# Rounding normalised feature tiles from the banks and sharing the normalisation between VectorE and ScalarE

## The chip, the core and the metric

The kernel runs on one core of a Trainium2 chip. The time is the device time of one launch in microseconds; it is read as the median of several runs. The engines have short names: PE (TensorE, matmuls and transposes; PEld are its weight loads), DVE (VectorE), ACT (ScalarE), POOL (GpSimd), SP (SyncE, which issues most DMAs). SBUF is the on-chip memory, and PE writes into eight banks of 128x512 f32.

## The reference

Two residual layers of an encoder, over 512 tokens (4 tiles of 128) with 1024 features (8 feature tiles of 128), all in f32:

```
for layer in range(2):
    mix = even_mixer(x) if layer == 0 else odd_mixer(x)      # GLA + windowed attention / gated DeltaNet
    x = layer_norm(ALPHA * x + mix, ln1_g, ln1_b)
    x = layer_norm(ALPHA * x + (silu(x @ w_gate) * (x @ w_up)) @ w_down, ln2_g, ln2_b)

def layer_norm(x, g, b):
    mu = mean(x); xc = x - mu
    return xc * rsqrt(mean(xc * xc) + 1e-5) * g + b
```

Each mixer is an input projection, the recurrence or attention, and an output projection of 1024 x 1024; the feed-forward width is 2816.

## The kernel before

Every f32 product is made of three matmuls: an operand is cut into a rounded high part and the low part that is left (x = x_hi + x_lo, w = w_hi + w_lo), and PE adds hi·hi, hi·lo and lo·hi into one bank (`mm3`). Weights come in blocks of 1 MB into two buffers `w_raw`; ACT rounds a block to `w_hi` in two pieces (line 823), POOL subtracts for `w_lo` in two pieces (line 681). Each engine has its own program in written order, and they meet at semaphores only: `full(e, key)` waits for a bank to be filled (on DVE and ACT it drains the engine first), `taken` for a bank to have been read.

Around a layer norm (i = 1, 2, 3; the fourth ends the kernel) there is a handover:

1. As PE finishes each token tile t of the last product, DVE adds it to ALPHA·x in `x_tm` (line 1234), takes statistics (1236, 1216), ACT takes the root (839), DVE the reciprocal (1191), and DVE normalises the row's two halves (1207). The normalising of a tile stands behind the adding of the next one.
2. PE transposes the four tiles into eight banks ("xT", i, k), one per feature tile k (`turn_x`, line 1816).
3. The norm's g and b are applied per feature as scale and bias. ACT makes x_hi of k = 0 from its bank (line 830). For every k, DVE writes f_ab, the unrounded feature tile, into one of four buffers (line 1174); for k = 1 to 7 ACT rounds x_hi from f_ab (line 834). The low part f_ab - x_hi is made by DVE for even k (line 1164) and by POOL for odd k (line 688).
4. `fm_block(..., fresh=i)` is PE's first weight block after the norm, two output tiles n: for each k, hi·hi and hi·w_lo for both n (1695, 1696), then the products with x_lo two tiles behind (1700). The banks of the two outputs are those of k = 1 and k = 0.

Before step 3, ACT rounds the next weight block (`split_to(... + 1)`), and POOL makes the first half of its w_lo ahead of the odd low parts, the second half behind them. After layer norm 2, ACT issues three DMAs between the two, among them `ba_w`, which PE needs in `few_columns` (line 1722) right after the fresh block. After a handover POOL also brings x_tm to the normalised x·g + b, one token tile in each of four weight blocks (794, 797), while SP loads the blocks that follow.

The end of a mixer: tiles 0 to 2 of the output projection's first half fill gaps of the mixer (`FILLERS`, `TAIL_FILLERS`, `LAST_FILLERS`). In layer 0 the last two fillers are done with k = 0 to 3 as `part_of` (high parts first, then the products with w_lo), k = 4 to 7 with `tile_of` (all three products at each k, so that each waits for w_lo). Then the last token tile is transposed (`turn_o`, line 1830). In layer 1 the filler `ahead` is cut in pieces around the transposes of the last OO, which DVE scales head by head (line 1634). The second half of the projection follows as `tm_group(("mix", layer, 1))`.

Of the kernel before, what the change touches and what calls it, by code (L numbers as in the profile page):

```python
# [286 lines left out]
def trunk_kernel(nc, A, out):  # L287
# [8 lines left out]
    with ctx:  # L296
# [31 lines left out]
        rstd = sb("rstd", [P, NT])  # L328
        TH = NT * GDN_H
# [181 lines left out]
        for b, (name, k0, nk, width, _) in enumerate(blocks):  # L511
# [19 lines left out]
            "eye_landed", "x_landed", "ln_landed", "warm_ready", "w_first_hi", "w_first_lo", "x_hi_ready", "x_lo_even", "x_lo_odd", "z_norm", "half_stats", "ln_stat", "ln_var",  # L531
# [143 lines left out]
        def _(pool):  # L675
# [8 lines left out]
            def low_parts(i):  # L684

                for k in range(1, KD, 2):
                    pool.wait_ge(s["x_hi_ready"], KD * i + k + 1)
                    pool.tensor_tensor(x_lo[:, k, :], f_ab[:, k % 4, :], x_hi[:, k, :].bitcast(F32), ALU.subtract)\
                        .then_inc(s["x_lo_odd"], 1)
# [74 lines left out]
            for b in range(2, NB):  # L764
# [39 lines left out]
        def _(act):  # L804
# [21 lines left out]
            def round_x(i):  # L826
# [151 lines left out]
            split_to(first_block[("gate", 0, 0)] + 1)  # L978
            round_x(1)
# [4 lines left out]
            split_to(first_block[("conv", KD)] + 1)  # L984
# [5 lines left out]
            round_x(2)  # L990
# [138 lines left out]
            split_to(first_block[("gate", 1, 0)] + 1)  # L1129
            round_x(3)  # L1130
# [6 lines left out]
        def _(dve):  # L1137
# [19 lines left out]
            def round_x(i):  # L1157
# [9 lines left out]
                for k in (1, 0, *range(2, KD)):  # L1167
                    full(dve, ("xT", i, k))
                    if k == 0:
                        dve.wait_ge(s["x_hi_ready"], KD * i + 1)  # L1170
# [5 lines left out]
                    if k % 2 == 0 and k > 0 or k == KD - 1:  # L1176
                        low((k - 1) // 2 * 2)
# [9 lines left out]
            def layer_norm(i, group, layer):  # L1187

                def normalise(t):
# [447 lines left out]
            filler(NT - 1, 3)  # L1637
# [10 lines left out]
        def _(pe):  # L1648
# [35 lines left out]
            def fm_block(b, keys, fresh=None, width=P):  # L1684
# [3 lines left out]
                for k in range(KD) if fresh is not None else ():  # L1688
# [38 lines left out]
            def tm_group(name, wait_k, src=xcols, kt=KD, in_turn=False, tiles=range(NT), pair_last=False):  # L1727
# [3 lines left out]
                while b < NB and blocks[b][0] == name:  # L1731
# [6 lines left out]
                    waited = -1  # L1738
                    for kk, t in steps:
# [470 lines left out]
```

## Time and profile before

| | us |
|---|---|
| median of 3 runs | 1258.07 (1258.04 to 1260.04) |
| the profiled execution's own time | 1257.68 |
| its span in the trace | 1255.87 |
| PE busy | 1232.8 |
| POOL, DVE, ACT busy | 602.8, 449.1, 442.0 |

The page shows one execution. Busy time counts an engine's instructions; a wait is shown in brackets as idle time before an instruction with what released it. The chain that ended last consists of PE by 91%, so the places that matter are those where PE waits.

### The profile page before, as it was taken

The page shows a single profiled execution, that of the slowest core. Times are in us where ns is not written, and L with a number is a line of the kernel's source. Part 1 is how long each engine was busy: PE and PEld are TensorE (multiplying, and loading weights), DVE is VectorE, ACT ScalarE, POOL GpSimd, SP SyncE. Part 2 cuts the span into 40 slices and gives each one's busy share as a digit, 9 for nine tenths or more (in the row PEclk, how much of TensorE's full clock was granted, in tenths as well). Part 3 has the DMA queues.
Part 4 walks back from the last instruction along what each step waited for, and adds up shares of the span by engine and source line. Part 5 has one row for each costly group of instructions (what it writes and reads, how often), then busy time and mean ns, then how long its engine had stood idle before and what let it go on. Part 6 is the DMA issues. An engine that isn't in the chain of part 4 may idle for free.

```text
span 1255.9 us, 17125 instructions
## 1 busy us (share of the span) xinstructions
PE 1232.8 (98%) x7112; PEld 1011.2 (81%) x7112; DVE 449.1 (36%) x769; ACT 442.0 (35%) x661; POOL 602.8 (48%) x292
## 2 busy tenths in 40 slices
PE   9999998999999999999999999999999999999997
PEld 7878776888888888886777889887688888888885
DVE  5557526311111000127778845663621111010105
ACT  4167724222222221214544456542422222221111
POOL 4243444944444343446743347444694444435341
PEclk9999999999999999999999999999999999999999
DMA  9221041333233233231344243124133233323231
GB/s 321 91 68 68 23 147 44 124 102 99 75 97 98 87 126 124 101 101 48 103 116 120 75 127 94 27 69 134 34 107 109 86 101 101 101 84 135 83 101 67
DMA packets 106065, 122.96 MB, mean 98 GB/s; under 512 B 18947, under 2 KB 80581, under 8 KB 105989
## 3 DMA queue, kind: packets, MB, share of 16 engines
q1 hardware_dynamic: 98244, 118.56, 29.7%
q10 hardware_dynamic: 7744, 3.32, 1.0%
q8 instruction: 56, 0.92, 0.3%
q14 instruction: 21, 0.16, 0.0%
HBM read 117.93 MB, written 3.70 MB: 97 GB/s over the span
## 4 chain that ended last, share of the span: by engine, by line
PE 91%; DVE 4%; DVEq 2%; POOL 1%; issue 1%; ACT 1%; ACTq 0%
PE bank L1661 27%; PE bank L1663 27%; PE bank L1662 27%; PE bank L2062 3%; DVEq L471 2%; DVE f_ab L1174 1%; POOL w_lo L681 1%; DVE stats L1236 1%; DVE x_tm L1234 1%; PE bank L2171 1%; PE bank L1722 1%; PE bank L1894 1%; PE bank L2008 0%; PE bank L2154 0%; DVE x_tm L1197 0%
## 5 line engine op out<-in xcount | busy, mean ns | idle before, releaser
L681 POOL TENSOR_TENSOR w_lo<-w_raw,w_hi 128x1024 fp32r<-128x1024 f32 (+1 forms) x200 | 469.9, 2371 | 525.7 <-ACT w_hi L823 525.5
L1661 PE MATMUL bank<-x_hi,w_hi 128*128 128x512 f32 x880 | 344.3, 391 | 0.0
L1662 PE MATMUL bank<-x_lo,w_hi 128*128 128x512 f32 x880 | 342.5, 389 | 0.0
L1663 PE MATMUL bank<-x_hi,w_lo 128*128 128x512 f32 x880 | 342.5, 389 | 0.0
L823 ACT ACTIVATE w_hi<-w_raw 128x1024 fp32r<-128x1024 f32 (+1 forms) x200 | 196.3, 1032 | 210.0 <-issue 161.3
L1661 PEld LDWEIGHTS bank<-x_hi,w_hi 128*128 128x128 f32 x880 | 165.2, 188 | 35.2 <-issue 0.8
L1663 PEld LDWEIGHTS bank<-x_hi,w_lo 128*128 128x128 f32 x880 | 165.2, 188 | 34.4
L1662 PEld LDWEIGHTS bank<-x_lo,w_hi 128*128 128x128 f32 x880 | 165.2, 188 | 34.0
L1243 DVE TENSOR_TENSOR f_ab<-bank,f_ab 128x512 f32<-128x512 f32 x44 | 30.4, 692 | 363.7 <-PE bank L1663 363.7
L1663 PE MATMUL bank<-w_hi,h_lo 128*128 128x512 f32 x352 | 136.9, 389 | 0.0
L1661 PE MATMUL bank<-w_hi,h_hi 128*128 128x512 f32 x352 | 136.9, 389 | 0.0
L1662 PE MATMUL bank<-w_lo,h_hi 128*128 128x512 f32 x352 | 136.9, 389 | 0.0
L1661 PE MATMUL bank<-w_hi,x_hi 128*128 128x512 f32 (+1 forms) x312 | 121.9, 391 | 2.1 <-POOL w_lo L681 2.1
L1663 PE MATMUL bank<-w_hi,x_lo 128*128 128x512 f32 (+1 forms) x312 | 118.4, 379 | 0.0
L1662 PE MATMUL bank<-w_lo,x_hi 128*128 128x512 f32 (+1 forms) x312 | 118.2, 379 | 0.0
L1234 DVE SCALAR_TENSOR_TENSOR x_tm<-x_tm,bank 128x512 f32<-128x512 f32 x32 | 22.0, 688 | 251.4 <-PE bank L1663 249.8
L862 ACT ACTIVATE h_hi<-f_ab 128x512 fp32r<-128x512 f32 x44 | 27.8, 632 | 187.4 <-DVE f_ab L1243 187.4
L1661 PEld LDWEIGHTS bank<-w_hi,h_hi 128*128 128x128 f32 x352 | 66.1, 188 | 13.8
L1662 PEld LDWEIGHTS bank<-w_lo,h_hi 128*128 128x128 f32 x352 | 66.1, 188 | 13.7
L1663 PEld LDWEIGHTS bank<-w_hi,h_lo 128*128 128x128 f32 x352 | 66.1, 188 | 13.7
L857 ACT ACTIVATE f_ab<-bank 128x512 f32<-128x512 f32 x44 | 26.3, 598 | 142.9 <-PE bank L1663 140.5
L1661 PEld LDWEIGHTS bank<-w_hi,x_hi 128*128 128x128 f32 x312 | 58.7, 188 | 15.4 <-POOL w_lo L681 3.8
(284 smaller groups left out, 1243.3 us busy)
## 6 DMA issues: line engine op xcount, KB each, us to landing
w_raw<-ffn_w_gate_dram SPq DMA_DIRECT2D x22, 1024.0 KB, 5.4
w_raw<-ffn_w_up_dram SPq DMA_DIRECT2D x22, 1024.0 KB, 5.3
w_raw<-ffn_w_down_dram SPq DMA_DIRECT2D x20, 1024.0 KB, 5.0
w_raw<-od_w_in_dram SPq DMA_DIRECT2D x16, 1024.0 KB, 5.9
w_raw<-ev_w_in_dram SPq DMA_DIRECT2D x8, 1024.0 KB, 5.6
w_raw<-ev_w_out_dram SPq DMA_DIRECT2D x4, 1024.0 KB, 5.2
w_raw<-od_w_out_dram SPq DMA_DIRECT2D x4, 1024.0 KB, 5.2
x_fm<-x_fm_dram SPq DMA_DIRECT2D x8, 256.0 KB, 6.8
```

What stands on the lines that cost most here:

```text
L471: e.drain()
L681: pool.tensor_tensor(w_lo[:, b % 2, c], w_raw[:, b % 2, c], w_hi[:, b % 2, c].bitcast(F32), ALU.subtract).then_inc(w_lo_ready, 1)
L823: act.activation(w_hi[:, i % 2, c], w_raw[:, i % 2, c], ACT.Copy).then_inc(w_hi_ready, 1)
L857: take(act.activation(f_ab[:, j, :], bank(("gate", layer, f + j))[:, :], ACT.Silu), ("gate", layer, f + j))
L862: act.activation(h_hi[:, f + j, :], f_ab[:, 2 + j, :], ACT.Copy).then_inc(s["h_hi_ready"], 1)
L1174: take(dve.tensor_scalar(f_ab[:, k % 4, :], src, lnc[:, gcol + k:gcol + k + 1], lnc[:, gcol + 16 + k:gcol + 17 + k], ALU.mult, ALU.add), ( ...
L1234: take(dve.scalar_tensor_tensor(cols, cols, ALPHA, bank(key)[:, :], ALU.mult, ALU.add), key)
L1243: take(dve.tensor_tensor(f_ab[:, 2 + f % 2, :], bank(("up", layer, f))[:, :], f_ab[:, f % 2, :], ALU.mult), ("up", layer, f))
L1661: pe.matmul(out_ap, st[0], mv_[0], start=start, stop=False)
L1662: pe.matmul(out_ap, st[0], mv_[1], start=False, stop=False)
L1663: return pe.matmul(out_ap, st[1], mv_[0], start=False, stop=stop)
L2062: return pe.matmul(o, a, b_, start=True, stop=True)
```

## The change

ACT reads the banks itself for k = 2 to 7 and makes x_hi from them (its own scale and bias); it also writes f_ab for k = 3, 5, 7, while DVE writes it for k = 1 and the even k only, each followed at once by its low part. ACT normalises the second half of every token tile, with a factor -mean·rstd that DVE computes into `nm_rstd`; the transposes of k = 4 to 7 wait for it by a semaphore of its own. The next weight block is rounded in two parts (`split_part`), the first between x_hi 2 and x_hi 3, the second behind all; POOL makes the first half of its w_lo between the low parts 3 and 5. The three DMAs of layer norm 2 come behind all that. On PE, the fresh block takes k = 0 and k = 1 of one output before the other output; the end of mixer 0 takes k = 4 to 7 of two fillers with high parts first; mix half 1 begins with k = 0, 1 without w_lo (`late=2`); a tile of the projection waits only for the parts of the transposed tile that it reads; at the end of mixer 1 `ahead` is cut 6 + 2 around the first transposes, and the two halves are transposed apart, with DVE's add of a filler between the two.

```diff
+            def low_parts(i, b):
+
+                pool.wait_ge(s["z_norm"], NT * i)
                 for k in range(1, KD, 2):
+                    if k == 5:
+                        split_lo(b, (0,))
                     pool.wait_ge(s["x_hi_ready"], KD * i + k + 1)
+                    taken(pool, ("xT", i, k))
...
-                    pool.wait_ge(s["z_norm"], 2 * NT * turned[b])
-                    split_lo(b + 1, (0,))
-                    low_parts(turned[b])
+                    low_parts(turned[b], b + 1)
...
+            def split_part(b, j):
+
+                assert split[0] == b
+                if j == 0:
+                    act.wait_ge(w_landed[b % 2], 16 * (b // 2 + b % 2))
+                    act.wait_ge(*block_end[b - 2])
+                    low_weights_all(act, b - 2)
+                act.activation(w_hi[:, b % 2, pieces(b)[j]], w_raw[:, b % 2, pieces(b)[j]], ACT.Copy).then_inc(w_hi_ready, 1)
+                split[0] += j
+
+            def round_x(i, b):
 
                 gcol = 32 * ((i + 1) % 2) + 8 * ((i - 1) // 2)
                 full(act, ("xT", i, 0))
                 act.activation(x_hi[:, 0, :], bank(("xT", i, 0))[:, :], ACT.Identity, scale=lnc[:, gcol:gcol + 1],
                                bias=lnc[:, gcol + 16:gcol + 17]).then_inc(s["x_hi_ready"], 1)
-                for k in range(1, KD):
-                    taken(act, ("xT", i, k))
-                    act.activation(x_hi[:, k, :], f_ab[:, k % 4, :], ACT.Copy).then_inc(s["x_hi_ready"], 1)
+                taken(act, ("xT", i, 1))
+                act.activation(x_hi[:, 1, :], f_ab[:, 1, :], ACT.Copy).then_inc(s["x_hi_ready"], 1)
+                for k in range(2, KD):
+                    if k == 3:
+                        split_part(b, 0)
+                    full(act, ("xT", i, k))
+                    scale, bias = (lnc[:, c + k:c + k + 1] for c in (gcol, gcol + 16))
+                    act.activation(x_hi[:, k, :], bank(("xT", i, k))[:, :], ACT.Identity, scale=scale,
+                                   bias=bias).then_inc(s["x_hi_ready"], 1)
+                    if k % 2:
+                        if k > 4:
+                            low_part_there(act, i, k - 4)
+                        take(act.activation(f_ab[:, k % 4, :], bank(("xT", i, k))[:, :], ACT.Identity, scale=scale,
+                                            bias=bias), ("xT", i, k))
+                split_part(b, 1)
 
             def layer_norm(i):
+                def normalise(t):
+                    act.wait_ge(s["nm_ready"], NT * (i - 1) + t + 1)
+                    act.activation(x_tm[:, t, 512:D], x_tm[:, t, 512:D], ACT.Identity, scale=rstd[:, t:t + 1],
+                                   bias=nm_rstd[:, t:t + 1]).then_inc(s["z_act"], 1)
+
                 for t in range(NT):
                     act.wait_ge(s["ln_var"], NT * (i - 1) + t + 1)
                     act.activation(rstd[:, t:t + 1], mv[:, t, 1:2], ACT.Sqrt, bias=eps[:, 0:1])\
                        .then_inc(s["ln_stat"], 1)
+                    if i < 4 and t:
+                        normalise(t - 1)
+                if i < 4:
+                    normalise(NT - 1)
...
-            split_to(first_block[("gate", 0, 0)] + 1)
-            round_x(1)
+            round_x(1, first_block[("gate", 0, 0)] + 1)
...
-            split_to(first_block[("conv", KD)] + 1)
+            round_x(2, first_block[("conv", KD)] + 1)
 
             act.dma_start(ba_w[:, :, :], A["od_w_in"][0][:, BA0:BA0 + SB].rearrange("(k p) n -> p k n", p=P))\
                .then_inc(s["ba_landed"], 16)
             for dst, c0, n in ((o_upto, 0, P), (o_negt, P, P)):
                 act.dma_start(dst[:, :], A["c_odd"][:, c0:c0 + n]).then_inc(consts, 16)
-            round_x(2)
...
-                for k in (1, 0, *range(2, KD)):
+                for k in (1, *range(0, KD, 2)):
                     full(dve, ("xT", i, k))
-                    if k == 0:
-                        dve.wait_ge(s["x_hi_ready"], KD * i + 1)
+                    if k != 1:
+                        dve.wait_ge(s["x_hi_ready"], KD * i + k + 1)
                     if k >= 4:
                         low_part_there(dve, i, k - 4)
                     src = bank(("xT", i, k))[:, :]
                     take(dve.tensor_scalar(f_ab[:, k % 4, :], src, lnc[:, gcol + k:gcol + k + 1],
                                            lnc[:, gcol + 16 + k:gcol + 17 + k], ALU.mult, ALU.add), ("xT", i, k))
-                    if k % 2 == 0 and k > 0 or k == KD - 1:
-                        low((k - 1) // 2 * 2)
+                    if k != 1:
+                        low(k)
...
-                    for h in range(2):
-                        c = slice(h * 512, (h + 1) * 512)
-                        dve.tensor_scalar(x_tm[:, t, c], x_tm[:, t, c], mv[:, t, 0:1], rstd[:, t:t + 1],
-                                          ALU.subtract, ALU.mult).then_inc(s["z_norm"], 1)
+                    dve.scalar_tensor_tensor(nm_rstd[:, t:t + 1], mv[:, t, 0:1], -1.0, rstd[:, t:t + 1],
+                                             ALU.mult, ALU.mult).then_inc(s["nm_ready"], 1)
+                    dve.tensor_scalar(x_tm[:, t, 0:512], x_tm[:, t, 0:512], mv[:, t, 0:1], rstd[:, t:t + 1],
+                                      ALU.subtract, ALU.mult).then_inc(s["z_norm"], 1)
...
-            filler(NT - 1, 3)
+                if hg == 0:
+                    filler(NT - 1, 3)
...
+                def high(k, n):
                     weights_there(b, k)
                     pe.wait_ge(s["x_hi_ready"], KD * fresh + k + 1)
-                    x = xcols(k, ALL)
+                    ps, w, x = fill(keys[n]) if k == 0 else bank(keys[n]), weights(b, k, n * P, P), xcols(k, ALL)
+                    pe.matmul(ps[:, :], w[0], x[0], start=k == 0, stop=False)
+                    pe.matmul(ps[:, :], w[1], x[0], start=False, stop=False)
+
+                for k in range(KD) if fresh is not None else ():
                     for n in range(len(keys)):
-                        ps = fill(keys[n]) if k == 0 else bank(keys[n])
-                        w = weights(b, k, n * P, P)
-                        pe.matmul(ps[:, :], w[0], x[0], start=k == 0, stop=False)
-                        pe.matmul(ps[:, :], w[1], x[0], start=False, stop=False)
+                        if k == 0:
+                            high(0, n)
+                            high(1, n)
+                        elif k > 1:
+                            high(k, n)
...
+                    waited = late - 1 if k0 == 0 else -1
+                    for kk in range(late) if k0 == 0 else ():
+                        if kk % (nk // 2) == 0:
+                            pe.wait_ge(w_hi_ready, split_count(b, kk // (nk // 2)))
+                        wait_k(kk)
+                        for t in tiles:
+                            ps = fill((*name, t)) if kk == 0 else bank((*name, t))
+                            hi = weights(b, kk, 0, width)[0]
+                            pe.matmul(ps[:, 0:width], src(kk, tile_cols[t])[0], hi, start=kk == 0, stop=False)
+                            pe.matmul(ps[:, 0:width], src(kk, tile_cols[t])[1], hi, start=False, stop=False)
+                    for kk in range(late) if k0 == 0 else ():
+                        weights_there(b, kk)
+                        for t in tiles:
+                            pe.matmul(bank((*name, t))[:, 0:width], src(kk, tile_cols[t])[0], weights(b, kk, 0, width)[1],
+                                      start=False, stop=False)
...
-                if key[0] == "mix" and k0 == 0:
-                    for i in range(2):
+                if key[0] == "mix":
+                    for i in range(k0 // 4, (k1 + 3) // 4):
...
-                            pe.wait_ge(s["z_norm"], 2 * (NT * (i - 1) + t) + k // 4 + 1)
+                            pe.wait_ge(s[("z_norm", "z_act")[k // 4]], NT * (i - 1) + t + 1)
...
-            for key in TAIL_FILLERS[0]:
-                tile_of(key, 4, 8)
+            for low in (False, True):
+                for key in TAIL_FILLERS[0]:
+                    part_of(key, 4, 8, low)
...
             filler(NT - 1, 3, 7, 8)
-            tile_of(ahead, 0, 4)
-            turn_o(1, NT - 1)
-            tile_of(ahead, 4, 7)
+            tile_of(ahead, 0, 6)
+            turn_o(1, NT - 1, (0,))
+            tile_of(ahead, 6, 8)
+            turn_o(1, NT - 1, (1,))
...
-            tile_of(ahead, 7, 8)
```

ACT's order at the first handover, before: the four roots, the next weight block, then x_hi.

```order
L823 ACTIVATE w_hi<-w_raw 128x1024 x6
L839 ACTIVATE rstd<-mv,eps 128x1 x4
L823 ACTIVATE w_hi<-w_raw 128x1024 x2
L830 ACTIVATE x_hi<-bank,lnc 128x512
L834 ACTIVATE x_hi<-f_ab 128x512 x7
L857 ACT_TABLE_LOAD
```

And with the change, from the same place on:

```order
L869 ACTIVATE rstd<-mv,eps 128x1
L864 ACTIVATE x_tm<-x_tm,nm_rstd,rstd 128x512 x2
L843 ACTIVATE x_hi<-bank,lnc 128x512
L846 ACTIVATE x_hi<-f_ab 128x512
L852 ACTIVATE x_hi<-bank,lnc 128x512
L836 ACTIVATE w_hi<-w_raw 128x1024
L852 ACTIVATE x_hi<-bank,lnc 128x512
L857 ACTIVATE f_ab<-bank,lnc 128x512
L852 ACTIVATE x_hi<-bank,lnc 128x512 x2
L857 ACTIVATE f_ab<-bank,lnc 128x512
```

The block's rounding has moved from ahead of all x_hi into the row and behind it; ACT has taken over DVE's f_ab of the odd tiles.

DVE after the last statistics of the same norm, before (each f_ab is a TENSOR_SCALAR from a bank, each low part a TENSOR_TENSOR):

```order
L1191 RECIPROCAL rstd<-rstd 128x1
L1207 TENSOR_SCALAR x_tm<-x_tm,mv,rstd 128x512 x2
L1174 TENSOR_SCALAR f_ab<-bank,lnc 128x512 x3
L1164 TENSOR_TENSOR x_lo<-f_ab,x_hi 128x512
L1174 TENSOR_SCALAR f_ab<-bank,lnc 128x512 x2
L1164 TENSOR_TENSOR x_lo<-f_ab,x_hi 128x512
L1174 TENSOR_SCALAR f_ab<-bank,lnc 128x512 x2
L1164 TENSOR_TENSOR x_lo<-f_ab,x_hi 128x512
```

With the change:

```order
L1222 RECIPROCAL rstd<-rstd 128x1
L1236 SCALAR_TENSOR_TENSOR nm_rstd<-mv,rstd 128x1
L1238 TENSOR_SCALAR x_tm<-x_tm,mv,rstd 128x512
L1205 TENSOR_SCALAR f_ab<-bank,lnc 128x512 x2
L1195 TENSOR_TENSOR x_lo<-f_ab,x_hi 128x512
L1205 TENSOR_SCALAR f_ab<-bank,lnc 128x512
L1195 TENSOR_TENSOR x_lo<-f_ab,x_hi 128x512
```

One f_ab instead of two stands ahead of each low part after the first.

## Rows read from the trace of the kernel before

**Rows 1.** The page's engines: busy us, share of the span, instructions.

```profile
PE 1232.8 (98%) x7112; PEld 1011.2 (81%) x7112; DVE 449.1 (36%) x769; ACT 442.0 (35%) x661; POOL 602.8 (48%) x292
```

**Rows 2.** Stretches: length, busy PE, PEld, DVE, ACT, POOL, granted clock, DMA.

```profile
195.79:216.00 20.21, 17.06 (x82) 12.19 (x81) 15.97 (x23) 8.70 (x13) 8.60 (x6) 1.00 0.01 2
563.93:583.88 19.95, 17.08 (x82) 12.01 (x81) 16.82 (x24) 7.52 (x12) 8.70 (x6) 1.00 0.08 20
842.30:856.95 14.65, 13.48 (x62) 10.14 (x60) 8.64 (x20) 4.87 (x8) 2.45 (x2) 1.00 0.01 1
878.64:898.50 19.86, 16.99 (x83) 12.22 (x82) 15.96 (x23) 8.73 (x13) 8.61 (x6) 1.00 0.00 2
```

**Rows 3.** PE's timeline, first handover: start, duration, instruction, [idle before <- releaser].

```profile
196.02 0.93 PE L1816 MATMUL bank<-eye,x_tm 128*128 128x128 f32 x7
...
213.58 0.50 PE L1695 MATMUL bank<-x_hi,w_hi 128*128 128x512 f32 x1 [0.86 <-ACT x_hi L834]
...
216.00 0.39 PE L1661 MATMUL bank<-x_hi,w_hi 128*128 128x512 f32 x1
...
219.63 0.39 PE L1662 MATMUL bank<-x_lo,w_hi 128*128 128x512 f32 x1
```

**Rows 4.** ACT's timeline, first handover.

```profile
198.31 1.99 ACT L823 ACTIVATE w_hi<-w_raw 128x1024 fp32r<-128x1024 f32 x2
200.38 0.78 ACT L830 ACTIVATE x_hi<-bank,lnc 128x512 fp32r<-128x512 f32 x1
...
212.90 0.63 ACT L834 ACTIVATE x_hi<-f_ab 128x512 fp32r<-128x512 f32 x1 [2.31 <-DVE f_ab L1174]
```

**Rows 5.** DVE's timeline, first handover.

```profile
196.41 0.69 DVE L1234 SCALAR_TENSOR_TENSOR x_tm<-x_tm,bank 128x512 f32<-128x512 f32 x1
...
199.05 0.15 DVE L1191 RECIPROCAL rstd<-rstd 128x1 f32<-128x1 f32 x1
199.24 1.00 DVE L1207 TENSOR_SCALAR x_tm<-x_tm,mv,rstd 128x512 f32<-128x512 f32 x2
200.34 0.81 DVE L1174 TENSOR_SCALAR f_ab<-bank,lnc 128x512 f32<-128x512 f32 x1
...
206.30 1.68 DVE L1164 TENSOR_TENSOR x_lo<-f_ab,x_hi 128x512 fp32r<-128x512 f32 x1
```

**Rows 6.** POOL's timeline, first handover.

```profile
200.32 2.37 POOL L681 TENSOR_TENSOR w_lo<-w_raw,w_hi 128x1024 fp32r<-128x1024 f32 x1 [9.04 <-ACT w_hi L823]
...
206.14 1.29 POOL L688 TENSOR_TENSOR x_lo<-f_ab,x_hi 128x512 fp32r<-128x512 f32 x1 [2.19 <-ACT x_hi L834]
```

**Rows 7.** PE's timeline, end of mixer 0.

```profile
153.03 2.18 PE L1800 MATMUL bank<-w_lo,x_hi 128*128 128x512 f32 x8
156.33 0.50 PE L1661 MATMUL bank<-w_hi,x_hi 128*128 128x512 f32 x1 [1.12 <-POOL w_lo L681]
...
158.65 0.50 PE L1661 MATMUL bank<-w_hi,x_hi 128*128 128x512 f32 x1 [0.67 <-POOL w_lo L681]
...
162.89 0.60 PE L1830 MATMUL bank<-eye,o_tm 128*128 128x128 f32 x4
```

**Rows 8.** ACT's timeline, end of mixer 0.

```profile
151.75 1.99 ACT L823 ACTIVATE w_hi<-w_raw 128x1024 fp32r<-128x1024 f32 x2
```

**Rows 9.** PE's timeline, end of mixer 1.

```profile
846.47 0.66 PE L1830 MATMUL bank<-eye,OO 128*128 128x128 f32 x4 [0.47 <-DVE OO L1634]
847.52 0.66 PE L1830 MATMUL bank<-eye,OO 128*128 128x128 f32 x4 [0.39 <-DVE OO L1634]
...
856.96 0.50 PE L1661 MATMUL bank<-w_hi,x_hi 128*128 128x512 f32 x1 [0.28 <-POOL w_lo L681]
```

**Rows 10.** ACT's DMA queue, second handover: start, duration of the issue.

```profile
566.39 0.38 ACTq L986 DMA_DIRECT2D ba_w<-od_w_in_dram  x1
```

**Rows 11.** The tile ba_w: its readers' durations, first and last start; DMA landing.

```profile
L1722 PE MATMUL bank<-x_hi,ba_w x16: 592/592/617, 583.9 to 585.2; 128*32 128x512 f32 x16
...
DMA to landing us min/median/max: 2.6/2.6/2.6
```

More of the change, by code:

```diff
@@ L328, in trunk_kernel @@
         rstd = sb("rstd", [P, NT])
+        nm_rstd = sb("nm_rstd", [P, NT])
         TH = NT * GDN_H
@@ L530, in trunk_kernel @@
         s = {n: sem(n) for n in (
-            "eye_landed", "x_landed", "ln_landed", "warm_ready", "w_first_hi", "w_first_lo", "x_hi_ready", "x_lo_even", "x_lo_odd", "z_norm", "half_stats", "ln_stat", "ln_var",
+            "eye_landed", "x_landed", "ln_landed", "warm_ready", "w_first_hi", "w_first_lo", "x_hi_ready", "x_lo_even", "x_lo_odd", "z_norm", "z_act", "nm_ready", "half_stats", "ln_stat", "ln_var",
             "x_affine", "out_sent", "act_step", "dve_step", "o_hi_ready", "h_hi_ready", "h_lo_ready",
@@ L824, in split_to @@
                     split[0] += 1
-            def round_x(i):
+            def split_part(b, j):
[7 more added lines that the diff above has]
+            def round_x(i, b):
                 gcol = 32 * ((i + 1) % 2) + 8 * ((i - 1) // 2)
@@ L1128, in _ @@
             layer_norm(3)
-            split_to(first_block[("gate", 1, 0)] + 1)
-            round_x(3)
+            round_x(3, first_block[("gate", 1, 0)] + 1)
             ffn(1)
@@ L1687, in fm_block @@
                 steps = [(n, k) for n in range(len(keys)) for k in range(KD)]
-                for k in range(KD) if fresh is not None else ():
+                def high(k, n):
                     weights_there(b, k)
                     pe.wait_ge(s["x_hi_ready"], KD * fresh + k + 1)
-                    x = xcols(k, ALL)
+                    ps, w, x = fill(keys[n]) if k == 0 else bank(keys[n]), weights(b, k, n * P, P), xcols(k, ALL)
+                    pe.matmul(ps[:, :], w[0], x[0], start=k == 0, stop=False)
+                    pe.matmul(ps[:, :], w[1], x[0], start=False, stop=False)
+                for k in range(KD) if fresh is not None else ():
                     for n in range(len(keys)):
-                        ps = fill(keys[n]) if k == 0 else bank(keys[n])
-                        w = weights(b, k, n * P, P)
-                        pe.matmul(ps[:, :], w[0], x[0], start=k == 0, stop=False)
-                        pe.matmul(ps[:, :], w[1], x[0], start=False, stop=False)
+                        if k == 0:
[3 more added lines that the diff above has]
+                            high(k, n)
                     for kl in [k - 2] * (k > 1) + [KD - 2, KD - 1] * (k == KD - 1):
@@ L1725, in few_columns, with tm_group @@
                 done(ins, key)
-            def tm_group(name, wait_k, src=xcols, kt=KD, in_turn=False, tiles=range(NT), pair_last=False):
+            def tm_group(name, wait_k, src=xcols, kt=KD, in_turn=False, tiles=range(NT), pair_last=False, late=0):
                 b = first_block[name]
@@ L1737, in tm_group @@
                         steps = [(kk, t) for t in tiles for kk in range(nk)]
-                    waited = -1
-                    for kk, t in steps:
+                    waited = late - 1 if k0 == 0 else -1
[13 more added lines that the diff above has]
+                                      start=False, stop=False)
+                    for kk, t in [(kk, t) for kk, t in steps if kk >= late or k0]:
                         if kk > waited:
@@ L1799, in part_of @@
                     if low:
-                        pe.matmul(ps[:, :], x_hi[:, k, x], lo, start=False, stop=False)
+                        ins = pe.matmul(ps[:, :], x_hi[:, k, x], lo, start=False, stop=k == KD - 1)
+                        if k == KD - 1:
+                            done(ins, key)
                     else:
@@ L1818, in turn_x, with turn_o @@
                             done(ins, ("xT", i, k))
-            def turn_o(layer, t):
-                for i in range(2 if layer else 1):
+            def turn_o(layer, t, parts=(0, 1)):
+                for i in parts if layer else (0,):
                     if layer == 0:
@@ L1835, in have @@
                     taken(pe, turned(layer, NT - 1, k // 4))
-                tm_group(("mix", layer, 1), have, in_turn=True)
+                tm_group(("mix", layer, 1), have, in_turn=True, late=2)
                 turn_x(2 * layer + 1)
```

1 line of the change is left out of this document (removed).

## The prediction

> **What bounds the kernel now.** I read the page's engine line first: the matmul engine PE is busy 98% of the span [rows 1], so a change can only pay where PE still stands. I then took one stretch per standstill with the windowed busy times. Three are the handovers in which a normalised x is transposed and split again, from the last matmul before to the first of the next weight block: 20.21, 19.95 and 19.86 us (the next block begins at 216.00 in the first) [rows 2, 3]. PE's work in one is 32 transposes and 48 matmuls. A matmul step is 0.227 us (sixteen from 216.00 to 219.63), a transpose 0.11 when nothing is waited for (seven in 0.93, the last drawn out to 0.27) [rows 3]; with 0.23 for these short chains that is 3.5 + 11.0 = 14.5 us, so each handover holds some 5.5 us of waits. The windows make that look smaller (17.06 of 20.21 busy), because a matmul that ends a chain is drawn out to its modelled end. The other two standstills are the ends of the mixers: 162.89 - 153.03 us in layer 0, with two waits for POOL's w_lo [rows 7], and 842.30 to 856.95 in layer 1, with waits for DVE's OO and again for w_lo [rows 2, 9]. The granted clock is 1.00 in all of them [rows 2], so idle time is the whole stake.
>
> Who is late in a handover is read from three engine timelines. PE waits for ACT's x_hi, which waits for DVE's f_ab (2.31 us before the last one) [rows 3, 4]. DVE is the pacemaker: per pair of feature tiles it makes two f_ab of 0.81 us and one low part. That low part takes 1.68 us because it begins at 206.30, inside POOL's low part of 206.14 to 207.43, and ends 0.55 us after it [rows 5, 6]. So DVE needs about 3.55 us a pair, and PE only 12 x 0.23 = 2.8.
>
> **The change part by part, in the times of the first handover.**
>
> *Normalising.* DVE gives half of each tile to ACT: one pass of 0.50 us less, and one 128x1 instruction more, for which the nearest row is the reciprocal (0.15) [rows 5]. Before, it came 0.2 us late to the last tile (196.41, PE's last product being out at 196.2). Now it is in time, but the extra instruction gives most of that back for tile 2. Tile 3's halves run side by side. ACT's half is an operation the trace doesn't show; between 0.63 (copy from SBUF) and 0.78 (bank with scale and bias) [rows 4], I take 0.8 to be safe. It ends near 199.8, where DVE's second half ended at 200.24. Gain 0.3 us, bounds -0.3 (ACT's pass held by the next tile's root ahead of it) and 0.5.
>
> *The split of the next weight block.* 1.99 us on ACT stood ahead of the first x_hi and ended at 200.30 [rows 4]. Now nothing does: x_hi 0 starts at 199.95 instead of 200.38.
>
> Where the first half now stands, its wait for the landed block has x_hi 3 to 7 queued behind it, and all of PE's tiles behind those; at 198.31 the same wait held nothing up (POOL's w_lo, queued ahead of low parts 5 and 7, waits for it in turn).
>
> *High parts.* For tiles 2 to 7 ACT reads the bank itself: 0.78 us each by the row of x_hi 0, the same form [rows 4]. It adds three f_ab for the odd tiles (same reads, 0.63 to 0.78, I take 0.78) and half a split of 1.0 us between tiles 2 and 3. With 0.1 us for each drain, from x_hi 1 (it still waits for DVE's f_ab 1, at 200.86, and ends at 201.5) on: tile 2 by 202.4, half a split to 203.35, tile 3 by 204.2, f_ab 3 by 204.9, tiles 4 and 5 by 205.7 and 206.6, f_ab 5 by 207.3, tiles 6 and 7 by 208.1 and 209.0, f_ab 7 by 209.65. The last x_hi came at 213.53 [rows 4].
>
> *PE.* It starts at 200.9 instead of 201.30, does tiles 0 and 1 of one bank before the other bank is needed (no wait for its release), and from tile 2 on takes six matmuls a tile, 1.39 us. Tile 2's begin at 203.03, tile 3's at 204.43, then 205.8, 207.2, 208.6, 210.0: every x_hi above is there, the tightest (tile 3, 4) by 0.1 to 0.2 us. PE would be through with all but the last low part at 211.84.
>
> *Low parts.* DVE now has three f_ab fewer in its way, POOL keeps the odd ones, with the first w_lo half (2.37 us) between parts 3 and 5. POOL: part 3 to 206.3, w_lo to 208.7, part 5 from 209.25 to 210.5, part 7, behind DVE's part 6, to 212.35. DVE (a low part that meets POOL's instruction ends 0.55 after it, one that doesn't is given 0.7): parts 0, 2 and 4 by 203.4, 205.1 and 209.25 (behind w_lo), part 6 by 211.05. PE wants them in order at 204, 206.75, 209.5 and 211.4, so only part 7 is late, and two matmuls follow it: the next block begins at 212.8 instead of 216.00, a gain of 3.2 us. The other two handovers were 0.26 and 0.35 us shorter before, and have the same work now: 2.9 and 2.85. Bounds for each: about 0, if an instruction of ACT's chain costs twice its row, and 3.9, if no low part is late.
>
> *The DMA of ba_w* (second handover) is issued after ACT's chain instead of before it. It went out at 566.39, took 2.6 us to land, and PE needed it at 583.9 [rows 10, 11]. In first-handover times it now goes out between the last x_hi's dispatch (208.2) and f_ab 7's end (209.65), is there by 212.3 at the latest, and PE wants it at 212.8: cost 0; at most 0.9 if the half split must end first.
>
> *End of mixer 0.* PE stood before two of its 24 second-half matmul groups until w_lo's halves were there, 156.33 and 158.65 [rows 7]. Now the 16 matmuls that need only w_hi (ready at 153.74 [rows 8]) come first: 154.9 + 16 x 0.23 = 158.6, the 8 with w_lo end at 160.4, and both halves are in place by then. The transposes follow at 160.4, not 162.89: 2.4 us, bounds 0 and 2.5.
>
> *End of mixer 1.* From 842.3, PE has 51 matmuls and 8 transposes until mix half 1 begins: 11.7 + 1.1 = 12.8 us, where it took 14.6. The waits were 0.47 and 0.39 for OO (the second is in the same place one transposition later) and 0.28 for w_lo, with a refill of 0.1 to 0.2 after each [rows 9]. Six more matmuls ahead of the first transposes and six between the two halves cover OO; the add and its statistics that DVE now does between the halves (twice 0.69, the first by its row [rows 5], the second taken to cost the same) delay the second to 849.1, which leaves about 0.3. Mix half 1 may begin without w_lo. Gain 1.6 us, bounds 0 and 1.8.
>
> *Sum:* 3.2 + 2.9 + 2.85 + 2.4 + 1.6 = 12.95 us off the profiled execution's 1257.68 (span 1255.87 and 1.8 around it). The median of the runs shown is 0.4 higher, 1258.07; I take 12.9 off that: **1245.2 us**.
>
> **Rivals.**
>
> *Part 7 before part 6.* Both low parts become ready near 210.5, one on POOL, one on DVE, and only one can run. If POOL's goes first, part 7 is there at 211.8, part 6 0.55 later at 212.35, and PE still has four matmuls after it: the next block begins at 213.3, 0.5 us later in each handover, and the time is 1246.7. For: POOL's part 7 needs only f_ab 7 (209.65), DVE's needs its own f_ab first. Against: POOL is still at part 5 then, and DVE has been waiting behind it. The Trainium skill (SBUF — State Buffer, section "Who interferes with whom") says that a VectorE instruction with two SBUF inputs and a GpSimd instruction that reads SBUF exclude each other, and that the second to issue waits for the whole of the first; the trace agrees with it in DVE's 1.68 us [rows 5, 6], and by it this rival is the case whenever POOL issues first.
>
> *ACT takes DVE's place as pacemaker.* Its chain in a handover grows to about 13.6 us of instructions. If each costs 1.0 instead of 0.78 (drains of 0.2 that nothing hides), the last x_hi comes at 210.75 and part 7 at 213.05: the handovers gain 2.2 rather than 3, and the tails 3.5: 1248. At double durations they gain nothing much, and only the tails stay: 1254. For: seven of its instructions follow a drain. Against: x_hi 0's row, which is drained as well.
>
> *Given back in the weight queue, slower.* After each handover POOL passes four weight blocks, each with two x_tm passes over 128x1024, taken at w_lo's price, and two w_lo halves of 2.37 [rows 6]: 9.5 us against PE's 48 x 0.227 = 10.9. PE comes 3.2 us earlier, POOL 2.5, so the slack of the first of them falls by 0.7. If lock waits brought POOL's instructions above 2.7 us, POOL would set the pace; at 3.1 it costs 1.5 us in each of 12 blocks, 18 us, and the time is 1263. Against: 2.37 in the row.
>
> *No effect in the handovers:* ACT's reads of the banks slow DVE's or PE's own; only the tails' 4 us remain, 1254.
>
> **How the numbers follow.** Forecast 0.48 (its own range 1242.5 to 1246); part 7 first, 1246.7, 0.22; ACT as pacemaker at 1248 to 1250.5, 0.18; only the tails, 1254, 0.06; no gain that can be told, 0.03; slower by the weight queue, 0.03. What a measurement of this kernel can tell from no change is about 0.2%, 2.5 us: faster 0.94, same 0.03, slower 0.03. The range goes from all five places at their upper bounds (15.3 us, and 0.2 in each normalisation: 1242.2) to the far end of the third case: 1242 to 1250.5.
>
> **What would show it.** Right: three handovers of about 17 us, the last x_hi within 9.1 us of x_hi 0's start, PE's only wait longer than 0.3 us after tile 2 in front of the last low parts; no wait for w_lo at the end of mixer 0; no x_lo of DVE over 2.5 us. Wrong: gaps before x_hi in every tile (ACT), a wait of PE for ba_w, or waits for w_lo in the blocks after a handover.

## The result, and the profile after

The kernel after takes 1250.94 us (median of 4 runs, 1250.86 to 1251.61), the one before, run beside it, 1258.09 us: 0.9941 of the time, interval 0.9923 to 0.9958. The forecast was 1245.2 us in a range of 1242.0 to 1250.5. The sign was right; of the 12.9 us forecast, 7.1 came.

The page's engines [rows 1] after:

```profile
PE 1235.4 (99%) x7112; PEld 1012.3 (81%) x7112; DVE 437.1 (35%) x760; ACT 459.4 (37%) x682; POOL 605.7 (48%) x292
```

PE has as many instructions as before, in a span 6.8 us shorter (1249.06), and yet it is busy 2.6 us *more*. Work that only lost waits doesn't get busier; keep that line in mind.

The three handovers in the trace after, between the same two matmuls as in [rows 2] (length; busy PE, PEld, DVE, ACT, POOL; granted clock; DMA):

```profile
193.35:210.25 16.90, 15.93 (x82) 12.38 (x81) 12.66 (x19) 13.51 (x19) 9.07 (x6) 1.00 0.01 2
561.74:578.73 16.99, 16.01 (x83) 12.22 (x81) 12.98 (x19) 12.27 (x18) 9.16 (x6) 1.00 0.09 18
871.64:888.53 16.89, 15.92 (x83) 12.40 (x81) 12.65 (x19) 13.52 (x19) 9.05 (x6) 1.00 0.00 1
```

Against 20.21, 19.95 and 19.86 us that is what was forecast ("about 17 us"). The timelines of the first one, engine by engine (start, duration, instruction, idle before and releaser), follow the plan closely; everything lies 2.44 us earlier, because the end of mixer 0 already was (0.07 of it is the program's earlier start). PE [rows 3]:

```profile
198.48 0.47 PE L1724 MATMUL bank<-x_hi,w_hi 128*128 128x512 f32 x1 [0.34 <-DVE f_ab L1205]
...
208.46 1.07 PE L1737 MATMUL bank<-x_lo,w_hi 128*128 128x512 f32 x4
209.69 0.72 PE L1737 MATMUL bank<-x_lo,w_hi 128*128 128x512 f32 x2 [0.16 <-POOL x_lo L693]
210.25 0.40 PE L1693 MATMUL bank<-x_hi,w_hi 128*128 128x512 f32 x1
```

ACT [rows 4], from its normalising to the last high part:

```profile
195.69 1.54 ACT L864 ACTIVATE x_tm<-x_tm,nm_rstd,rstd 128x512 f32<-128x512 f32 x2
197.41 0.78 ACT L843 ACTIVATE x_hi<-bank,lnc 128x512 fp32r<-128x512 f32 x1 [0.18 <-PE bank L1869]
...
199.76 1.05 ACT L836 ACTIVATE w_hi<-w_raw 128x1024 fp32r<-128x1024 f32 x1
...
204.82 1.64 ACT L852 ACTIVATE x_hi<-bank,lnc 128x512 fp32r<-128x512 f32 x2
```

DVE [rows 5] and then POOL [rows 6]:

```profile
204.14 2.62 DVE L1195 TENSOR_TENSOR x_lo<-f_ab,x_hi 128x512 fp32r<-128x512 f32 x1
206.95 0.81 DVE L1205 TENSOR_SCALAR f_ab<-bank,lnc 128x512 f32<-128x512 f32 x1 [0.19 <-DVE x_lo L1195]
207.79 0.69 DVE L1195 TENSOR_TENSOR x_lo<-f_ab,x_hi 128x512 fp32r<-128x512 f32 x1
```

```profile
203.79 2.42 POOL L682 TENSOR_TENSOR w_lo<-w_raw,w_hi 128x1024 fp32r<-128x1024 f32 x1
206.15 3.48 POOL L693 TENSOR_TENSOR x_lo<-f_ab,x_hi 128x512 fp32r<-128x512 f32 x2
```

The last x_hi ends at 206.46, 9.05 us after x_hi 0 began; DVE's part 6 (207.79) goes between POOL's two parts; PE's last wait, for part 7, is 0.16 us.

The two mixers' ends, in PE's timeline [rows 7, 9]; the first two rows are mixer 0's (eight low parts of the weights at once, then the transposes), the other two mixer 1's:

```profile
158.66 1.98 PE L1851 MATMUL bank<-w_lo,x_hi 128*128 128x512 f32 x8
160.47 0.60 PE L1883 MATMUL bank<-eye,o_tm 128*128 128x128 f32 x4
```

```profile
842.10 0.60 PE L1883 MATMUL bank<-eye,OO 128*128 128x128 f32 x4
...
843.93 0.66 PE L1883 MATMUL bank<-eye,OO 128*128 128x128 f32 x4
```

None of the four has a wait ahead of it. So far every place gives what the sum said. Put side by side, from the starts of the same matmuls in both traces (the windows of [rows 2] are up to 0.03 us wider):

| stretch | before, us | after, us | gain | forecast |
|---|---|---|---|---|
| to the end of mixer 0 (first handover's start) | 195.79 | 193.35 | 2.44 | 2.4 |
| handovers 1, 2, 3 | 20.21, 19.94, 19.83 | 16.90, 16.99, 16.89 | 3.31 + 2.95 + 2.94 | 3.2 + 2.9 + 2.85 |
| mixer 1 | 294.76 | 292.91 | 1.85 | 1.6 |
| gate and up, both layers | 228.48, 228.48 | 228.53, 228.53 | -0.10 | 0 |
| **down, both layers** | **119.46, 119.45** | **122.96, 122.96** | **-7.01** | **0** |
| last normalisation | 9.47 | 9.04 | 0.43 | 0 |
| span | 1255.87 | 1249.06 | 6.81 | 12.95 |

The five places of the forecast gave 13.5 us, and the down projections took back 7.0. They have no waits in either trace. The windows of the first down stage, from its first matmul to the transposes behind it, before and then after:

```profile
444.48:564.17 119.69, 119.69 (x529) 99.05 (x528) 13.45 (x25) 25.95 (x29) 54.84 (x24) 1.00 0.34 110
```

```profile
438.78:561.97 123.19, 123.19 (x530) 99.13 (x528) 12.99 (x25) 27.29 (x31) 54.73 (x24) 1.00 0.32 107
```

PE busy throughout, granted clock 1.00, the same DMA and the same work beside it; but 528 steps take 119.69 us before (226.7 ns each) and 123.19 after (233.3). The view of the tile h_hi, which is the stationary operand there (a weight load of 128 columns for each matmul with 512 columns of w), shows that every one of them is affected (duration min/median/max, first and last start). Before, then after:

```profile
L1661 PEld LDWEIGHTS bank<-w_hi,h_hi x352: 187/188/188, 444.3 to 1245.7; 128*128 128x128 f32 x176
L1661 PE MATMUL bank<-w_hi,h_hi x352: 389/389/389, 444.5 to 1246.0; 128*128 128x512 f32 x176
```

```profile
L1693 PEld LDWEIGHTS bank<-w_hi,h_hi x352: 187/188/188, 438.5 to 1239.3; 128*128 128x128 f32 x176
L1693 PE MATMUL bank<-w_hi,h_hi x352: 392/395/396, 438.8 to 1239.5; 128*128 128x512 f32 x176
```

The code of these matmuls was not changed. What the whole diff does change for them is one line far away, a declaration that the excerpts ahead of the prediction leave out: `nm_rstd = sb("nm_rstd", [P, NT])`. `sb` hands out SBUF in order, each tile rounded up to 32 bytes, so every tile behind that line lies 32 bytes further on, h_hi and h_lo among them (h_hi at byte 119712 of a partition instead of 119680). w_hi, w_lo, x_hi and x_lo are allocated ahead of it and stay.

### The profile page after: what moved, and what is told of

Its sections match the earlier page's. It is cut to its first block, busy times and chain, and to the rows that moved or that the text cites. A ratio compares the mean times of both kernels' runs of the same rounds, so it can differ in the third digit from the quotient of the medians.

```text
span 1249.1 us, 17159 instructions
## 1 busy us (share of the span) xinstructions
PE 1235.4 (99%) x7112; PEld 1012.3 (81%) x7112; DVE 437.1 (35%) x760; ACT 459.4 (37%) x682; POOL 605.7 (48%) x292
## 2 busy tenths in 40 slices
DMA packets 106064, 122.96 MB, mean 98 GB/s; under 512 B 18946, under 2 KB 80580, under 8 KB 105988
## 4 chain that ended last, share of the span: by engine, by line
PE 94%; DVE 2%; POOL 1%; issue 1%; ACTq 1%; ACT 1%; DVEq 0%; POOLq 0%
PE bank L1693 28%; PE bank L1694 27%; PE bank L1695 27%; PE bank L2116 3%; POOL x_lo L693 1%; ACTq L472 1%; PE bank L1947 1%; PE bank L2225 1%; PE bank L1759 1%; PE bank L2062 0%; PE bank L2208 0%; PE bank L1883 0%; PE bank L1907 0%; DVE x_tm L1228 0%; DVE stats L1267 0%
## 5 line engine op out<-in xcount | busy, mean ns | idle before, releaser
L826 ACT ACTIVATE w_hi<-w_raw 128x1024 fp32r<-128x1024 f32 x194 | 190.3, 1031 | 212.6 <-issue 165.2
L1693 PE MATMUL bank<-w_hi,x_hi 128*128 128x512 f32 (+1 forms) x288 | 112.2, 389 | 0.0
L1695 PE MATMUL bank<-w_hi,x_lo 128*128 128x512 f32 (+1 forms) x288 | 109.0, 378 | 0.0
L1694 PE MATMUL bank<-w_lo,x_hi 128*128 128x512 f32 (+1 forms) x288 | 108.9, 378 | 0.0
L1482 DVE SCALAR_TENSOR_TENSOR KH<-bank,convw,KH 128x511 f32<-128x511 f32 (+2 forms) x72 | 53.9, 749 | 30.3 <-ACT KH L1034 27.0
```

The lines of the kernel that those rows point to most:

```text
L826: act.activation(w_hi[:, i % 2, c], w_raw[:, i % 2, c], ACT.Copy).then_inc(w_hi_ready, 1)
L1482: ins = dve.scalar_tensor_tensor(dst, bank(key)[:, 0:SEQ - back], convw[:, tap:tap + 1], dst, ALU.mult, ALU.add)
L1693: pe.matmul(out_ap, st[0], mv_[0], start=start, stop=False)
L1694: pe.matmul(out_ap, st[0], mv_[1], start=False, stop=False)
L1695: return pe.matmul(out_ap, st[1], mv_[0], start=False, stop=stop)
```

## The experiments

All times are medians; the kernel before, run beside each group, took 1257.8 to 1258.0 us. The first four ask whether the address is it.

**after_pad64**: 32 unused bytes more, so h lies 64 off its old place.

```diff
         nm_rstd = sb("nm_rstd", [P, NT])
+        spare = sb("spare", [P, NT])
```

> The kernel after, with one more 32-byte tile that nothing uses behind nm_rstd, so that h_hi and h_lo lie 64 bytes behind their places in the kernel before instead of 32; no instruction is changed. Theory A (address): a stationary operand that begins 32 bytes off a multiple of 64 makes each matmul of the down projections 6.7 ns longer (226.7 to 233.4); here it is gone, each down stage is 119.6 us again instead of 123.1, and the time is 1250.9 - 7.0 = 1243.9 us. Theory B (what the earlier handover brings, for instance other traffic beside the down stage or the chip's own limit on TensorE): 233 ns stays, 1250.9 us.

Measured: 1250.96 us, ratio 0.9946 (0.9933 to 0.9958). No change, which looks like theory B. The next two say otherwise.

**before_32** and **before_64**: the kernel before, with nothing but 32 or 64 unused bytes.

```diff
         rstd = sb("rstd", [P, NT])
+        spare = sb("spare", [P, NT])        # before_64: 4 * NT
```

> The kernel before with nothing but a 32-byte tile that nothing uses behind rstd. Theory A: matmuls of both down stages go from 226.7 to 233.4 ns, 2 x 528 x 6.7 ns = 7.1 us, so 1265.1 us. Theory B: 1258.1 us, since no instruction is changed.

> Control: the kernel before with a 64-byte tile that nothing uses in the same place, so that every later tile moves but keeps its place within 64 bytes. Theory A: 1258.1 us, matmuls at 226.7 ns. If any move costs, or if 128 bytes is what counts, as much as the 32-byte move: 1265 us. Theory B: 1258.1 us.

Measured: 1264.40 us, ratio 1.0052 (1.0040 to 1.0065), and 1264.28 us, 1.0052 (1.0039 to 1.0064). An unused tile costs 6.5 us with every instruction as it was, so theory B is out, and so is 64 bytes as the distance that is harmless. The window of before_32's first down stage, from its first to its last matmul (527 steps of 233.3 ns):

```profile
444.62:567.58 122.96, 122.96 (x528) 98.99 (x527) 13.37 (x25) 25.94 (x29) 54.71 (x24) 1.00 0.33 107
```

**after_x32**: the same with x, the operand of the other matmuls; h lies 64 off here.

```diff
+        spare = sb("spare", [P, NT])
         x_hi = sb("x_hi", [P, KD, SEQ], F32R)
```

> The kernel after with a 32-byte tile that nothing uses ahead of x_hi: x_hi, x_lo, x_tm and eye now begin 32 bytes off a multiple of 64, h_hi and h_lo on a multiple. x is the moving operand of the gate and up blocks and the stationary one of some 650 matmuls of the mixers. Theory A with stationary operands alone: down stages 119.6 us, the mixers' matmuls with x stationary at 233 ns, about 1250.9 - 7.0 + 4.4 = 1248.3 us. Theory A for both operands: the 2112 matmuls of gate and up at 233 ns as well, 14 us more, and the mixers' blocks: about 1266 us. Theory B: 1250.9 us.

Measured: 1272.36 us, ratio 1.0113 (1.0097 to 1.0128), so both operands' roles count: "about 1266" took h for unharmed, and its 7 us on top make 1273. The tile view of x_hi has x moving, against 389/389/504 in the trace after (with x stationary, `bank<-w_hi,x_hi` in the mixers, the median goes from 389 to 396 as well):

```profile
L1694 PE MATMUL bank<-x_hi,w_hi x880: 392/396/506, 41.6 to 1138.0; 128*128 128x512 f32 x176
```

Not every width pays. The same run has 96 matmuls with x stationary and only 256 columns of w, one after the other early in mixer 0. Their windows from the first to the last start (95 steps), in the kernel after (x and w 0 apart modulo 256) and then here (32 apart):

```profile
28.78:40.17 11.39, 11.39 (x96) 11.38 (x95) 10.98 (x21) 2.60 (x5) 5.79 (x3) 1.00 0.74 250
```

```profile
30.14:41.38 11.24, 11.24 (x97) 11.23 (x95) 10.86 (x19) 2.60 (x5) 4.95 (x2) 1.00 0.60 189
```

That is 119.9 ns a step at 0 and 118.3 at 32: not longer, but 1.7 ns shorter.

**after_hole**: the change, with no tile moved.

```diff
-        rstd = sb("rstd", [P, NT])
-        nm_rstd = sb("nm_rstd", [P, NT])
+        rstds = sb("rstds", [P, 2 * NT])
+        rstd, nm_rstd = rstds[:, 0:NT], rstds[:, NT:2 * NT]
```

> The kernel after, with nm_rstd in the 16 bytes that rstd leaves free of its 32, so that every other tile lies where it lay in the kernel before; no instruction is changed. Theory A2 (what counts is that an operand of a matmul begins on a multiple of 128 bytes; 32 and 64 off cost the same 6.7 ns): both down stages 119.6 us again, 1250.9 - 7.0 = 1243.9 us. Theory B (233 ns comes from what runs beside the down stage after the change): 1250.9 us.

Measured: 1244.61 us, ratio 0.9893 (0.9880 to 0.9907), 0.6 us from the forecast for the change itself. Its first down stage, first to last matmul, and its first handover:

```profile
439.22:558.67 119.45, 119.45 (x528) 98.91 (x527) 12.93 (x25) 27.00 (x31) 54.83 (x24) 1.00 0.34 109
...
193.79:210.69 16.90, 15.93 (x82) 12.40 (x81) 12.63 (x19) 13.52 (x19) 9.05 (x6) 1.00 0.01 3
```

The handover of the kernel after, to the hundredth, and the down stage of the kernel before. No instruction differs from the kernel after, so the 7 us hang on where the tiles lie.

**before_h128**: h alone moved, by 128 bytes.

```diff
-        here[0] = ARENA
+        here[0] = ARENA + 128
         h_hi = sb("h_hi", [P, KF, SEQ], F32R)
```

> The kernel before with h_hi, h_lo and the two tiles behind them moved by 128 bytes, the rest in place. Before the move all operands of 512-column matmuls lie 128 bytes off a multiple of 256, so this tells 128 from 256. Theory A2: 227 ns in both down stages, 1257.8 us. If the period is 256 bytes or any move of h costs: 233 ns, 1264.3 us.

Measured: 1263.98 us, ratio 1.0046 (1.0034 to 1.0059): theory A2, multiples of 128, fell as well. The first down stage, 232.4 ns a step:

```profile
444.40:566.87 122.47, 122.47 (x528) 99.28 (x527) 13.35 (x25) 25.94 (x29) 54.86 (x24) 1.00 0.33 107
```

In the kernel before w_hi begins at byte 32896, x_hi at 65664 and h_hi at 119680 of a partition, all three 128 above a multiple of 256. So either that place itself counts or only that they share it.

**before_all64**: everything moved together.

```diff
-        base = (nc.sbuf_base + 63) // 64 * 64
+        base = (nc.sbuf_base + 63) // 64 * 64 + 64
```

> The kernel before with every tile 64 bytes further on, so that the places of w, x and h among each other stay and only the absolute ones change. Theory H1 (each operand by itself has to begin 128 bytes off a multiple of 256, where w, x and h all lay before): every 512-column matmul at 233 ns, some 4000 of them by 6.7 ns, about 1284 us, less what waits hide. Theory H2 (the stationary and the moving operand have to agree in their place within 256 bytes): nothing changes, 1257.9 us.

Measured: 1258.00 us, ratio 0.9999 (0.9991 to 1.0008). H1 is out by 26 us: moving everything by 64 bytes cost nothing, so here the absolute place didn't count, only how the operands lie to each other. The first down stage, 226.7 ns a step:

```profile
444.45:563.90 119.45, 119.45 (x528) 98.91 (x527) 13.21 (x25) 25.95 (x29) 54.85 (x24) 1.00 0.35 110
```

**before_h256**: as before_h128, with `ARENA + 256`.

> The kernel before with h_hi, h_lo and the two tiles behind them moved by 256 bytes, the rest in place. H1 and H2 with a period of 256 bytes: 226.7 ns in both down stages, 1257.9 us. If the period is 512 or more, or if any move of h against w costs: 232 to 233 ns, 1264 us.

Measured: 1258.05 us, ratio 1.0000 (0.9991 to 1.0009): 256 bytes are harmless where 128 are not.

All of it in one table (distance from w_hi, as far as it differs from a multiple of 256 bytes):

| kernel | h | x | step in down | time, us |
|---|---|---|---|---|
| before; before_h256; before_all64 | 0 | 0 | 226.7 ns | 1258 |
| before_32 | 32 | 0 | 233.3 | 1264.4 |
| before_64 | 64 | 0 | 233.3 | 1264.3 |
| before_h128 | 128 | 0 | 232.4 | 1264.0 |
| after | 32 | 0 | 233.3 | 1250.9 |
| after_pad64 | 64 | 0 | 233.3 | 1251.0 |
| after_x32 | 64 | 32 | 233.3 | 1272.4 |
| after_hole | 0 | 0 | 226.7 | 1244.6 |

The remaining four take the forecast's own terms apart.

**tails_only**: the kernel before with the reorderings of the mixers' ends.

```diff
-                tile_of(key, 4, 8)
+            for low in (False, True):
+                for key in TAIL_FILLERS[0]:
+                    part_of(key, 4, 8, low)
...
-                tm_group(("mix", layer, 1), have, in_turn=True)
+                tm_group(("mix", layer, 1), have, in_turn=True, late=2)
```

> The kernel before with the reorderings at the two mixers' ends alone (high parts of four fillers ahead of their low ones, late=2, the last tile in 6 and 2 parts with finer waits); no new tile. If the parts add up as read from the trace after: 1257.8 - 2.4 - 1.9 = 1253.5 us. Rival (the layer norm behind each end waits for something else, which only the new handover speeds up, so an earlier end is partly given back): 1255.5 us or more.

Measured: 1254.01 us, ratio 0.9967 (0.9954 to 0.9979): 3.9 us, forecast 4.0. The first handover behind it is as long as before (20.22 us), and the third, behind the end of mixer 1, too (19.84, was 19.83), so nothing of the earlier ends is given back there, and the rival fell:

```profile
193.99:214.21 20.22, 16.99 (x83) 12.19 (x81) 15.97 (x23) 8.72 (x13) 8.61 (x6) 1.00 0.01 2
```

**handovers_only**: the rest of the diff, with nm_rstd as in after_hole.

```diff
-                for k in range(1, KD):
-                    taken(act, ("xT", i, k))
-                    act.activation(x_hi[:, k, :], f_ab[:, k % 4, :], ACT.Copy).then_inc(s["x_hi_ready"], 1)
+                for k in range(2, KD):
+                    if k == 3:
+                        split_part(b, 0)
+                    full(act, ("xT", i, k))
...
```

> The kernel before with the change at the three handovers alone (high parts from the banks, ACT's half of the normalising, the next block's rounding between them, the order of the fresh block), the mixers' ends as before, nm_rstd in the free bytes of rstd so that no tile moves. As the predicted terms: 1257.9 - 8.95 = 1248.9 us; as the trace after reads: 1257.9 - 9.1 = 1248.8 us; as after_hole less tails_only: 1257.9 - 9.4 = 1248.5 us. Rival (handovers and ends depend on each other): 1247 or less, or over 1250.

Measured: 1248.90 us, ratio 0.9927 (0.9915 to 0.9940): 9.1 us, forecast 8.95. With the 3.9 of the ends that makes 13.0, and after_hole has 13.3: the two parts add up.

**split_ahead**: after_hole with the next block's rounding where it was.

```diff
-                    if k == 3:
-                        split_part(b, 0)
...
+                split_to(b)
                 full(act, ("xT", i, 0))
```

> after_hole with the rounding of the block behind the fresh one back at its old place, ahead of high part 0 on ACT (2 x 1.05 us) and ahead of the odd low parts on POOL. If ACT's high parts set the handover: each is later by 2.1 us, the last by 1.05, so 1 to 2.1 us per handover, 1247.6 to 1250.9 us, likeliest 1247.7. Rival (the end of the handover is set by the low parts of POOL and DVE, which then have w_lo out of their way): 1244.6 us.

Measured: 1246.70 us, ratio 0.9909 (0.9896 to 0.9923); the interval overlaps that of after_hole, so the trace has to say it: the handovers take 17.78, 17.86 and 17.77 us instead of 16.90, 16.99 and 16.91. The first one, as a window and in PE's timeline:

```profile
193.40:211.18 17.78, 15.37 (x83) 12.49 (x81) 12.67 (x19) 13.40 (x19) 9.48 (x6) 1.00 0.01 3
```

```profile
200.14 0.47 PE L1721 MATMUL bank<-x_hi,w_hi 128*128 128x512 f32 x1 [1.95 <-ACT x_hi L843]
...
209.82 1.52 PE L1734 MATMUL bank<-x_lo,w_hi 128*128 128x512 f32 x6
211.18 0.39 PE L1690 MATMUL bank<-x_hi,w_hi 128*128 128x512 f32 x1
```

All the waiting is now ahead of the first matmul (1.95 us instead of 0.34), and from there on PE runs without any. So 1.6 us come in at the front, 0.7 go again because nothing is late behind, and 0.88 us a handover stay, a little less than the 1 to 2.1 expected. ACT is late at the start of a handover, not at its end.

**after_all128**: after_hole, with the operands of mixer 1's small matmuls moved by 32 bytes.

```diff
         o_negt = sb("o_negt", [P, P])
-        o_own = sb("o_own", [P, P // SB])
...
         OO = sb("OO", [P, GDN_H, P])
+        o_own = sb("o_own", [P, P // SB])
```

> after_hole, and o_own (32 bytes) behind the last tile of mixer 1's arena instead of ahead of blocks_in, so that the tiles that mixer 1's delta-rule matmuls read (blocks_in, KH, GU, EE, GT, GA, TT, SS, M1, ST, OO) begin on multiples of 128 instead of 32 off. Theory A2 in proportion: some 350 matmuls of 128 columns at 109 ns instead of 112, at most 1 us less than after_hole, so 1242.9 to 1243.9 us. Rival (mixer 1 waits for DVE and POOL there, not for these matmuls): as after_hole, 1243.9 us.

Measured: 1244.32 us, ratio 0.9892 (0.9877 to 0.9907), not to be told from after_hole's 1244.61; the chains of mixer 1 don't gain by it. Nor do the matmuls: most read two tiles that moved together, or two that stayed, and those whose operands did move against each other, from 32 to 0 bytes modulo 256, are no faster. `bank<-ST,qkv` (128 columns) has a median step of 112 ns in both traces, and the 32 matmuls of x (512 columns) with the 32-column ba_w as stationary operand take 3.05 us from first to last start in both, and also in the kernel after, where the distance is 64. These matmuls are plain f32, those with w rounded (float32r), so this says nothing on width alone. The 109 ns of the forecast were not there to be had. These two are the fastest kernels here, 1.1% under the one before.

## Why the prediction was wrong

*Right, and in size:* the end of mixer 0 (2.4 forecast, 2.44 measured, 0.07 of that an earlier start), the handovers (8.95; 9.2 in the trace, 9.1 alone), the end of mixer 1 (1.6; 1.85). Inside the handover the times hold as well, if 2.44 is added to those of the trace after: x_hi 0 forecast at 199.95, at 199.85; the last x_hi ends at 209.0, at 208.90; part 7 at 212.35, at 212.07; the next block at 212.8, at 212.69. ACT's new operations cost what the nearest rows said: its half of a normalising 0.815 (taken as 0.8), a high part from the bank 0.78. ba_w stayed hidden: there is no wait ahead of its matmuls.

*Wrong in a detail:* "no x_lo of DVE over 2.5 us" failed by 0.12: part 4 took 2.62, from 204.14 behind POOL's w_lo (203.79 to 206.21), and ended 0.55 after it. The Trainium skill (SBUF — State Buffer, section "Who interferes with whom") says that only the port pair shared by VectorE and GpSimd causes contention, and that it is an exclusive lock; the trace agrees in these two instructions. The sign contradicted the working, which had that wait in (part 4 by 209.25, so 206.81 here; it ended at 206.76), and PE didn't feel it.

*The rivals:* part 7 did not go before part 6, but that was close: DVE's part 6 began at 207.79, POOL's part 7 at 207.88, and in the other two handovers 0.07 and 0.08 us lay between them; ACT did not become the pacemaker (its instructions took what was assumed within 0.05 us); the weight queue gave nothing back (gate and up are 0.05 us longer a layer).

*The step that failed* is one that the sum didn't have. The list of what the change adds named instructions, waits and a DMA, and left out the new tile; a tile of 16 bytes was silently costed at nothing. It moved h by 32 bytes against w, each of the 2 x 528 matmuls of the down projections became 6.6 ns longer, and 7.0 us were gone (6.6 net: the last normalisation, with its products arriving more slowly, is 0.43 shorter, 9.04 us; before_32 has 9.08 there). No row of the trace before shows that price, but that the tiles move was to be read in the whole diff, and a cost that no row bounds should have kept the range open. With that one term at its measured size the sum is 12.95 - 6.6, about 6.4, or 1251.7 us, within 0.8 of the measurement.

*Open:* why the place counts. That stationary and moving operand have to agree modulo 256 bytes fits every kernel of the table, but in each of them they move against other tiles too, and no run moves w alone; distances between 128 and 256 were not tried. It is shown for rounded (float32r) operands, 128-column weights and 512 moving columns only: with 256 columns the steps were 1.7 ns shorter at 32 bytes (after_x32), and mixer 1's plain f32 matmuls, of 128 columns or with ba_w, took the same (after_all128). Why is open too.

## What to carry to other kernels

A declaration is an edit too: where tiles are handed out in order, write down the address of every matmul operand before and after the change, and put a small new tile into a hole or behind the last operand, so that operands read together keep their distance modulo 256 bytes (the case shown is float32r, 128-column weights with 512 moving columns). When the waits that a change removed add up to more than the span lost, divide each unbroken stretch by its count of matmuls in both traces: a step of 233 ns instead of 227 shows in no list of waits.

## What the hardware showed that was not expected

A float32r matmul step with 128-column weights and 512 moving columns took 226.7 ns where the place of stationary and moving operand agreed modulo 256 bytes, and 232.4 to 233.3 ns where it was 32, 64 or 128 off, at a granted clock of 1.00 in all of them, with the weight loads' own records the same in the median (188 ns). It holds for h and x as the stationary and for x as the moving operand. It did not show with 256 moving columns (118.3 ns at 32 bytes against 119.9 at 0), nor in plain f32 matmuls of 128 (112 at both).

The Trainium skill (TensorE: Matmul & The Clock Gate, section "Step-by-step: what each phase is for") says that the weight load and the stream of the matmul have independent read ports, so that loading the next weights takes nothing from the running matmul. By that, before_32 would have taken the 1257.8 us of the kernel before; it took 1264.4, with no instruction changed and w and h at another distance in the stage that grew, so the measurement decides: here the step depends on where the two lie to each other. That the two reads get in each other's way would explain it, but no run shows that.
